# A two-block transformer kernel on one core: 128 value columns and 24 gate columns projected together instead of one after the other

## The reference, cut to what matters

```
h = modulate(rmsnorm(x, norm_mix_g[l]), sh1, sc1)
proj = h @ w_in
q_a, kv_a, gate_a, qkv_b, merge = jnp.split(proj, IN_SPLITS, axis=-1)
k_cmp, v_cmp, k_sel, v_sel, k_win, v_win = (kv_a[i] for i in range(6))
g_a = jax.nn.sigmoid(gate_a.reshape(B, S, G, R, 3).transpose(0, 2, 3, 1, 4))
```

## Time and profile before

| What | Value |
|---|---|
| Three timed runs | 1880.43, 1886.88, 1888.17 us |
| Span of the profiled execution | 1878.5 us |
| The profiled execution's own time | not recorded with it; the fastest timed run is 1.9 us above the span, the median 8.4 us |
| TensorE busy | 1726.9 us, 92% |
| TensorE weight loads (beside the matmuls) | 1178.8 us |
| VectorE busy | 803.2 us, 43% |
| ScalarE busy | 528.9 us, 28% |
| Mean granted TensorE clock | 0.977 |

### The profile page before, as it was taken

One profiled execution on the slowest core, in us unless ns is written; L12 is line 12 of the kernel. 1 busy time (PEld: TensorE's weight loads), 2 busy tenths in 40 slices (PEclk: granted clock), 3 DMA queues, 4 the chain that ended last, 5 costly groups with the idle time before them and its releaser, 6 DMA issues. The chain is left out here.

```text
span 1878.5 us, 20208 instructions
## 1 busy us (share of the span) xinstructions
PE 1726.9 (92%) x8167; PEld 1178.8 (63%) x8167; DVE 803.2 (43%) x1272; ACT 528.9 (28%) x890; POOL 48.4 (3%) x89
## 2 busy tenths in 40 slices
PE   2999989979979999999989999999799989898888
PEld 2887866636667888878768876758334434343346
DVE  4763457642462222255642275335423323232345
ACT  4312346731242222232433243324200000000036
POOL 0000000100000000000000000000200000000000
PEclk8999989999989999999989999999999999999999
DMA  9664121022422322221322111218699999999961
GB/s 349 217 258 147 46 96 40 2 90 90 136 89 86 94 90 90 90 101 68 134 68 90 45 46 45 90 45 346 252 422 424 427 427 428 426 426 426 428 275 45
DMA packets 87655, 351.75 MB, mean 187 GB/s; under 512 B 9910, under 2 KB 39266, under 8 KB 71561
## 3 DMA queue, kind: packets, MB, share of 16 engines
q1 hardware_dynamic: 85002, 346.08, 47.3%
q0 software_dynamic: 2560, 4.37, 0.7%
HBM read 346.03 MB, written 8.43 MB: 189 GB/s over the span
## 5 line engine op out<-in xcount | busy, mean ns | idle before, releaser
L547 DVE TENSOR_TENSOR arena<-ring,arena 128x1024 fp32r<-128x1024 f32 x120 | 146.9, 1225 | 243.2 <-ACT arena L596 224.0
L2651 PE MATMUL ex_h<-ring,u_big_tail 128*64 128x512 f32 x512 | 152.3, 603 | 12.6 <-DMA ring<-in_w 7.6
L552 PE MATMUL up_ps<-h_high,arena 128*128 128x512 f32 x352 | 139.4, 396 | 6.7 <-PEq L178 6.2
L553 PE MATMUL up_ps<-arena 128*128 128x512 f32 x352 | 139.9, 397 | 0.0
L554 PE MATMUL up_ps<-h_high,arena 128*128 128x512 f32 x352 | 139.7, 397 | 0.0
L596 ACT CAST arena<-ring 128x1024 fp32r<-128x1024 f32 x82 | 85.8, 1047 | 167.9 <-PE up_ps L554 88.9
L2651 PE MATMUL ex_h<-s_ab,u_big_tail 128*64 128x512 f32 x272 | 114.3, 596 | 2.4 <-DVE u_big_tail L2622 1.4
L2622 DVE TENSOR_TENSOR u_big_tail<-ex_x,vcol 128x512 f32<-128x512 f32 x32 | 20.6, 686 | 179.6 <-PE ex_x L2615 179.6
L2651 PEld LDWEIGHTS ex_h<-ring,u_big_tail 128*64 128x64 f32 x512 | 47.1, 138 | 76.4 <-issue 75.5
L2917 ACT ACTIVATE u_big_tail<-ex_h 128x512 f32<-128x512 f32 x16 | 9.6, 597 | 292.4 <-PE ex_h L2651 292.4
L552 PEld LDWEIGHTS up_ps<-h_high,arena 128*128 128x128 f32 x352 | 66.5, 189 | 23.4 <-issue 6.6
(11 more groups left out here) (576 smaller groups left out, 3582.0 us busy)
## 6 DMA issues: line engine op xcount, KB each, us to landing
ring<-in_w SPq DMA_DIRECT2D x42, 2048.0 KB, 32.6
s_ab<-in_w SPq DMA_DIRECT2D x32, 2048.0 KB, 31.9
ring<-in_w_in SPq DMA_DIRECT2D x19, 2048.0 KB, 8.2
ring<-in_w_ada SPq DMA_DIRECT2D x24, 1024.0 KB, 6.9
reg_a<-in_w SPq DMA_DIRECT2D x10, 2048.0 KB, 31.8
w1flat<-in_w SPq DMA_DIRECT2D x10, 2048.0 KB
ring<-in_w_ffn_gate SPq DMA_DIRECT2D x11, 1024.0 KB, 5.4
ring<-in_w_ffn_up SPq DMA_DIRECT2D x11, 1024.0 KB, 7.9
```

The lines of the kernel that those rows point to most:

```text
L547: return engine.tensor_tensor(lo, v, hi.bitcast(F32), ALU.subtract)
L552: nc.tensor.matmul(ps, x[0], y[0], start=start, stop=False)
L553: nc.tensor.matmul(ps, x[0], y[1], start=False, stop=False)
L2651: mm = nc.tensor.matmul(ps[half, :], xT[:, k, half], ws[j][:, k, cols], start=(k == 0), stop=(k == k_end - 1))
```

## The change

Tile 9 (`rows`, 128 columns, 4 token tiles) and tile 10 (`gate`, 24 columns, 4 token tiles) become two tiles of a new kind `both`. Each makes all 152 columns for two token tiles, the first for token tiles 0 and 1, the second for 2 and 3. The number of tiles, their banks and the engines that empty them stay the same, but each of the two is now emptied with two copies: 2 x 128 columns to the values and 2 x 24 columns to the gates.

```
-    tiles += [(2, 0, "dup", b.kk[1]), (2, P, "rows", b.vv[1]), (2, 2 * P, "gate", b.gate)]
+    tiles += [(2, 0, "dup", b.kk[1]), (2, P, "both", 0), (2, P, "both", 2)]
...
-                    n = P if kind == "rows" else 24
-                    for t in range(NT):
-                        mm = product_rows(nc, bank[:, t * n:t * n + n], b.hT, t, w[:, :, n0:n0 + n], KD)
+                    n, t0, t1 = (P, 0, NT) if kind == "rows" else (P + 24, to, to + 2)
+                    for t in range(t0, t1):
+                        at = (t - t0) * n
+                        mm = product_rows(nc, bank[:, at:at + n], b.hT, t, w[:, :, n0:n0 + n], KD)
...
-                last = copy(dst[:], bank[:, 0:NT * 24].rearrange("p (t n) -> p t n", t=NT))
+                both = bank[:, 0:2 * (P + 24)].rearrange("p (t n) -> p t n", t=2)
+                copy(b.vv[1][:, dst:dst + 2, :], both[:, :, 0:P])
+                last = copy(b.gate[:, dst:dst + 2, :], both[:, :, P:P + 24])
```

More of the change, by code:

```diff
@@ L735, in directs @@
     def directs(i):
-        return sum(t[2] in ("rows", "gate") for t in tiles[:i + 1])
+        return sum(t[2] in ("rows", "both") for t in tiles[:i + 1])
     b.acc2 = b.ring[:, 3]
@@ L780, in _ @@
         def _(pe):
-            for i, (c, n0, kind, _) in enumerate(tiles):
+            for i, (c, n0, kind, to) in enumerate(tiles):
                 if i >= NB and not (kind == "wide" and n0):
@@ L797, in _ @@
                         parts.pe_rows(pe, unit_of[i] + j, [ps[(i + t) % NB] for t in range(NT)], 2 * j)
-                if kind in ("rows", "gate"):
+                if kind in ("rows", "both"):
                     mm.then_inc(direct, 1)
```

## The result

The change makes the kernel slower. The changed kernel takes 1892.6 us in the median of 7 runs (1889.42 to 1893.97), the kernel before 1885.5 us in 7 runs beside it (1880.43 to 1888.17). The ratio is 1.0041, with an interval of 1.0029 to 1.0054. Forecast were 1885 us and a range up to 1890.5 us. The profiled execution after took 1892.7 us with a span of 1890.9 us; the span before was 1878.5 us. These two spans are 12.4 us apart, more than the medians, because single executions of one kernel scatter by several us.

A forecast was written before the change was run, and what follows sets the result against it. TensorE was taken as the bound, with VectorE's list and its loads next; 3.9 us gained at tile 13 less 2.0 us of half clock leaves about 2 us, so 1886.9 - 2.0 = 1885 us, range 1877 to 1890.5.

The forecast's parts named there:

- The price of the product: Tiles 9 and 10: 64 records of 152 columns at 0.135 us each, 8.6 us in all, with no clock fall.
- VectorE as the next holder: Before tile 13: VectorE's low part behind slab 10 holds TensorE idle about 5.0 us; tile 13 begins at 127.4, gaining 3.9 us.
- The half clock behind the gap: After the idle time before tile 13: TensorE's clock falls to 0.50, costing 1.5 to 2.5 us, taken as 2.0.
- All later stages start behind a barrier that TensorE reaches last, and the loads of the experts are issued when their buffers come free, so what is kept here is passed on: All stages after the first: the about 2 us kept there carries through, making the span 1876.5 us.
- The rival "slower": Later stages: starting 2 us sooner moves gaps into clock falls of 1.5 us or more each, up to 1891 us; chance 0.20.
- 2 us gain: First stage: about 2 us kept from tile 13's 3.9 us sooner start after the half clock's cost, below a 3.3 us ceiling.
- 9.4 us, which is about what a measurement of this kernel can tell from no change: Whole kernel: no case reaches 0.5% of the time, 9.4 us, so "same" got 0.86.

The follow-up runs named there:

- after_low_first_w64: Kernel after with 64 waits at the start and, in VectorE's steps 11 to 17, the next unit's low part ahead of the slab; 1874.21 us, ratio 0.9947.
- before_w128: Kernel before with 128 wait instructions added on TensorE at the program's start; 1894.24 us, ratio 1.0059.
- after_w128: Kernel after with 128 wait instructions added on TensorE at the program's start; 1884.43 us, ratio 1.0007.
- before_skip120: Kernel before with 120 instructions of waits added inside TensorE's spilled-token code, which is jumped over; 1894.53 us, ratio 1.0043.
- after_pad9: Kernel after with 9 unread matmuls (2.0 us) added behind the last tile of the first stage; 1888.01 us, ratio 1.0018.
- before_skip62: Kernel before with 62 instructions of waits added inside TensorE's spilled-token code, which is jumped over; 1891.19 us, ratio 1.0028.
- after_again: Kernel after, unchanged, run once more; 1892.12 us, ratio to the kernel before 1.0023.
- after_no_branch_w32: Kernel after without TensorE's spilled-token code and its branch, with 66 waits (32 instructions) at the start; 1882.74 us, ratio 1.0.

## Why the prediction was wrong, point by point

- **The price of the product: right.** 0.131 us a record against 0.135; tile 11 at 111.00 against 111.5; no fall of the clock in it. Tile 11 began 7.6 us sooner, of which 0.37 us stood already ahead of the product (102.26 against 102.63); the forecast was 7.1.
- **VectorE as the next holder: right.** The gap is 5.20 us against "about 5.0", released by line 547, and tile 13 begins 0.04 us from where it was put. `after_low_first_w64` shows that it was VectorE's order and not the load alone that held it.
- **The half clock behind the gap: right.** Clock 0.50 from 127 to 131, at a price of 1.9 us against 2.0, gone when the gap is filled. The next stage began 2.03 us sooner against "about 2 us". That the single pair of profiles meets it so closely is partly luck: the start of that stage differs by up to 5 us between profiles; the averages over six and eight profiles are 2.2 us apart.
- **"All later stages start behind a barrier that TensorE reaches last, and the loads of the experts are issued when their buffers come free, so what is kept here is passed on": this step failed.** It took the later stages to run as before, only sooner, and had no term for how TensorE's instructions arrive. The edit made TensorE's list 128 instructions shorter, which moved the packet borders under the jump some 1700 us later: it crosses two instead of one, and costs 6.15 us instead of 0.42. With the half clock behind it that is 8.4 us in the profiles, against the 2 us forecast as gain. Whether the 2 us arrive at that jump is not shown: the transposes ahead of it begin on average at 1808.1 in the eight profiles with the new first stage and at 1810.1 in the six with the old one, but they scatter by 9 to 12 us within each group. The edit's length carried the cost, not its work: `before_w128` has the loss without the change, `after_w128` the change without the loss, and `before_skip120` the loss from instructions that are never carried out.
- **The rival "slower": its sign was right, its mechanism wrong.** It put a slower kernel down to later clock falls. Those differ between two executions of one program, and `after_pad9`, with 2.0 us of work more in the first stage, still stalled and was still slower, 1.0018 [1.0003, 1.0033].
- **Is the 2 us gain in the whole time?** Not shown. Without the stall the change measures 1.0007 [0.9994, 1.002] with 128 instructions put back and 0.9996 and 0.9997 with 64, so it is no change that can be measured here. 2 us are 0.1%.
- **"9.4 us, which is about what a measurement of this kernel can tell from no change": too coarse.** The 7.1 us were told from none with 7 runs a side, by an interval of 1.0029 to 1.0054, and so were the 0.28% of `before_skip62`.

Open stays how TensorE asks for a packet in detail, and how much of the 6 us is due to DMA engines that are full of other loads. The runs bound the first: a border right behind a jump's target costs 4.25 to 4.4 us, one 74 instructions behind it (the kernel before) nothing. That the two packets it holds are the current and the next one fits every count that is not too close to tell, but was not tried in another program.

## What to carry to other kernels

An edit changes the length of an engine's instruction list, and where a later branch jumps over more than a packet's worth of code, that alone can cost some 8 us far from the edit, as it did here. So a difference between two versions is to be searched for over the whole span, first among the waits that are put down to "issue", and a version without a gain is worth one more run with its list brought to the old length. Long code that is rarely used is a risk where the engine that bounds the kernel jumps over it: without it, neither of the two placements tried stalled. And where TensorE gets faster and waits for another engine, look at that engine's order: with the low part ahead of the slab the kernel became 8.7 us faster than with the new product alone.

## What the runs showed of the hardware

- A branch of TensorE takes 0.42 to 0.51 us where its target is loaded and 6.08 to 6.63 us where it is not; the longest is that of `after_again`. The same branch takes 0.05 to 0.07 us on the other engines.
- TensorE's instructions arrive in packets of 16 KB, about one in 30 us in the experts' stage (1.08 MB in 66 packets over the span). With the DMA engines at 0.83 to 1.03, one that a branch had to wait for kept it 6.08 to 6.63 us.
- The Trainium skill's page "Runtime: NRT & Kernel Launch", in its section "Instruction fetch mechanics", calls the cost of passing a 16 KiB boundary mostly hidden. Of `after_no_branch_w32` that holds; with a jump just ahead of the border it was 4.25 to 4.4 us.
- A plain float32 matmul record costs 0.106 us with 24 moving columns, 0.114 with 128, 0.131 with 152 and 0.225 with 256, all at full clock: below 128 columns there is nearly nothing to save.
